# Row sums of the second norm one pair of weight pieces sooner, and two gate pieces loaded among the last projection's pieces

## The reference, cut to what matters

```
mod = silu(c) @ ada_w + ada_b                      # 6 x 1024: sh1, sc1, gt1, sh2, sc2, gt2
...
merged = gate_a * (o_a @ w_oa) + gate_b * (o_b @ w_ob)
x = x + gt1 * (merged @ w_out)
h = rms_norm(x, norm2_g) * (1 + sc2) + sh2
x = x + gt2 * hier_moe(h, router weights, w1, w3, w2)   # 32 experts, each token in 2 of them
out = rms_norm(x, final_norm_g)
```

## Time and profile before

| | |
|---|---|
| median of 3 runs | 700.7 us (698.7 to 700.85) |
| the profiled execution | 700.86 us, its span 699.0 us |
| granted TensorE clock, mean | 0.991 of 2.4 GHz |
| PE, PEld busy | 669.4 us (96%), 538.5 us (77%) |
| DVE, ACT, POOL busy | 420.1 us (60%), 264.8 us (38%), 71.4 us (10%) |
| HBM read | 195.35 MB |

### The profile page before, as it was taken

How to read it: one execution, slowest core, us unless ns; L and a number is a source line. 1 busy time by engine, 2 the same in 40 slices (tenths; PEclk the granted TensorE clock), 3 DMA queues, 4 the chain that set the end, 5 groups by cost and what they waited for, 6 DMA issues and landing times.

```text
span 699.0 us, 12784 instructions
## 1 busy us (share of the span) xinstructions
PE 669.4 (96%) x5402; PEld 538.5 (77%) x5402; DVE 420.1 (60%) x710; ACT 264.8 (38%) x373; POOL 71.4 (10%) x70
## 2 busy tenths in 40 slices
PE   8999999999999999999998999899999999999893
PEld 8999999998777777999988997675666666665441
DVE  4656788987866789977786678644333122221226
ACT  3346545557763624335552332312131121221003
POOL 0001000000003614300000000001112111111111
PEclk9999999999999999999999999999999999999998
DMA  8987764455343443346639976999999999999992
GB/s 363 423 353 243 298 248 175 130 177 191 121 157 130 161 142 121 122 140 253 241 108 397 410 280 249 423 421 418 419 397 418 421 421 421 419 418 418 420 355 95
DMA packets 31195, 201.23 MB, mean 288 GB/s; under 512 B 5047, under 2 KB 5431, under 8 KB 7970
## 3 DMA queue, kind: packets, MB, share of 16 engines
q1 hardware_dynamic: 27378, 193.27, 70.7%
q0 software_dynamic: 3760, 7.14, 2.8%
HBM read 195.35 MB, written 10.75 MB: 295 GB/s over the span
## 4 chain that ended last, share of the span: by engine, by line
PE 77%; DVE 9%; DMA 6%; ACT 3%; issue 2%; SPq 2%; DVEq 0%; POOL 0%; ACTq 0%; POOLq 0%
PE ps L1571 75%; DMA ring<-in_expert_pieces 4%; DVE ring_rounded L934 2%; DMA ring<-in_pieces 2%; ACT ring_rounded L644 2%; SPq L461 1%; PE ps L1988 1%; PE ps L1692 1%; DVE r_ct L1209 1%; DVE r_v L1209 1%; DVE r_xs_rounded L1239 1%; ACT sq L760 1%; DVE g_sb L1142 0%; DVE r_kq L1173 0%; DVE newton L920 0%
## 5 line engine op out<-in xcount | busy, mean ns | idle before, releaser
L934 DVE TENSOR_TENSOR ring_rounded<-ring,ring_rounded 128x2048 fp32r<-128x2048 f32 x60 | 136.8, 2291 | 38.8 <-ACT ring_rounded L644 38.5
L1571 PE MATMUL ps<-hT_rounded,ring_rounded 128*128 128x256 f32 x832 | 150.1, 286 | 1.1 <-ACT hT_rounded L658 1.1
L1571 PEld LDWEIGHTS ps<-hT_rounded,ring_rounded 128*128 128x128 f32 x832 | 129.2, 193 | 5.1 <-issue 3.9
L644 ACT CAST ring_rounded<-ring 128x2048 fp32r<-128x2048 f32 x60 | 114.1, 1906 | 34.4 <-PE ps L1571 18.8
L1571 PE MATMUL ps<-ring_rounded,hT_rounded 128*128 128x512 f32 x352 | 109.7, 393 | 0.9 <-DVE ring_rounded L934 0.9
L1571 PE MATMUL ps<-x_sb_rounded,ring_rounded 128*128 128x256 f32 x416 | 109.8, 284 | 0.0
L1571 PEld LDWEIGHTS ps<-x_sb_rounded,ring_rounded 128*128 128x128 f32 x416 | 77.3, 193 | 0.9 <-issue 0.2
L1571 PEld LDWEIGHTS ps<-ring_rounded,hT_rounded 128*128 128x128 f32 x352 | 64.3, 188 | 14.8 <-issue 1.4
L858 ACT ACTIVATE sq<-ps 128x128 f32<-128x128 f32 x32 | 8.9, 277 | 142.6 <-PE ps L1571 142.6
L1454 DVE TENSOR_TENSOR r_st<-ps,r_kq 128x512 f32<-128x512 f32 x32 | 22.1, 692 | 65.0 <-PE ps L1571 65.0
L603 POOL DMA_INDIRECT y_rows<-r_st,r_btm x29 | 28.5, 984 | 311.4 <-DVE r_st L1454 298.6
(11 more groups left out here) (336 smaller groups left out, 1002.9 us busy)
## 6 DMA issues: line engine op xcount, KB each, us to landing
ring<-in_pieces SPq DMA_DIRECT2D x66, 1024.0 KB, 5.0
ring<-in_expert_pieces SPq DMA_DIRECT2D x48, 1024.0 KB, 17.5
r_z<-in_expert_pieces SPq DMA_DIRECT2D x12, 1024.0 KB, 13.3
r_xs<-in_expert_pieces SPq DMA_DIRECT2D x12, 1024.0 KB, 12.5
r_v<-in_pieces SPq DMA_DIRECT2D x6, 1024.0 KB, 7.2
r_ct<-in_pieces SPq DMA_DIRECT2D x6, 1024.0 KB, 5.6
g_sb<-in_expert_pieces SPq DMA_DIRECT2D x6, 1024.0 KB, 17.2
r_st<-in_expert_pieces SPq DMA_DIRECT2D x6, 1024.0 KB, 17.9
```

The source lines that it names most:

```text
L644: nc.scalar.copy(high_of(p_), slot_of(p_)).then_inc(hi_ok, 1)
L934: nc.vector.tensor_tensor(low_of(p_), slot_of(p_), high_of(p_).bitcast(F32), ALU.subtract).then_inc(lo_ok, 1)
L1571: return nc.tensor.matmul(o, l, r, start=start, stop=stop)
```

## The change

Two things. DVE sums row pair 9 after the drain of `ob (1,0)` instead of `ob (1,1)`, and SP loads it accordingly when `ob (0,1)` has been read instead of `ob (1,0)`. And SP issues the first two gate pieces ahead of the load that waits for piece (1,0,1) of `ob`, which is that of `out` piece (1,0), instead of behind expert pieces 4 and 5.

```
-ROWS_AT = {("oa", 1, 1): 7, ("ob", 0, 1): 8, ("ob", 1, 1): 9}
+ROWS_AT = {("oa", 1, 1): 7, ("ob", 0, 1): 8, ("ob", 1, 0): 9}
...
-                if n >= LOADS and PIECES[n - LOADS] in (("ob", 0, 0, 1), ("ob", 1, 0, 1)):
+                if n >= LOADS and PIECES[n - LOADS] in (("ob", 0, 0, 1), ("ob", 0, 1, 1)):
                     piece_used(sp, PIECES[n - LOADS])
-                    load_rows(8 + PIECES[n - LOADS][1])
+                    load_rows(8 + PIECES[n - LOADS][2])
+                if n >= LOADS and PIECES[n - LOADS] == ("ob", 1, 0, 1):
+                    sp.wait_ge(start_row_read, 4 + len(ROW_PIECES))
+                    for p_q in GATE_ROWS[:2]:
+                        sp.dma_start(slot_of(p_q), piece_src(p_q)).then_inc(s_gate, 16)
                 load_piece(n, p_)
...
             load_moe(4)
             load_moe(5)
-            sp.wait_ge(start_row_read, 4 + len(ROW_PIECES))
-            for p_ in GATE_ROWS[:2]:
-                sp.dma_start(slot_of(p_), piece_src(p_)).then_inc(s_gate, 16)
             for p_ in GATE_ROWS[2:]:
                 load_piece(PIECE_AT[p_], p_)
...
                         if (name, i, h) in ROWS_AT:
-                            if (name, i) == ("ob", 1):
-                                before((("out", 0), 0))
+                            if name == "oa":
+                                split_to(SPLIT_AT["ob", 0, 0, 1] + 1)
                             rows_out(ROWS_AT[name, i, h])
```

## The result

Twelve runs of each kernel, in turn on one chip: 699.42 us before (698.32 to 702.1), 701.81 us after (700.46 to 703.78). The ratio is 1.0035, 95% interval 1.0022 to 1.0047: slower by 2.4 us (1.5 to 3.3). The forecast was no difference that can be measured, 700.5 us; 701.81 lies in its range, but the likeliest case was wrong. Two figures ahead of the result mislead a little: the median of three shown for before, 700.7, was 1.3 us above the one of twelve, and the profiled execution of before, 700.86 us, was 1.4 us above it. It lost TensorE's clock once more than that of after, from 60 to 68 us (granted 0.67 and 0.90 in two windows of 4 us, where after has 1.00). So after's profiled execution is 2.2 us ahead at 384 us (TensorE resumes at 383.55, in before at 385.72), and both spans are 699.0 us: the 2.2 us ahead are gone at the end.

What follows compares the result with a forecast made beforehand. The expert-weight stream was taken to set the end. TensorE 2.6 us late against 2.9 in hand gave -0.3 us on the profiled 700.86, and with the median 0.16 below the profiled time, 700.5; 8-in-10 range 697.6 to 703.4.

Steps and rivals of the forecast that it cites:

- 5.53 us at the router weights: DVE, before scaling the router weights: predicted to stand 5.0 us until their load lands at 429.8.
- 3.58 us at O3: TensorE, last projection's third piece: predicted to idle 3.6 us until DVE has split it at 433.7.
- the clock's fall: TensorE's granted clock, predicted to fall after the 3.6 us idle in the last projection, costing about 1.4 us.
- the new DMA hole before piece 16: Expert stream at some 465 to 468 us: earlier loads mostly given back as a hole before piece 16.
- how late TensorE is: TensorE's entry to the experts: predicted 2.6 us late, 1.2 plus 1.4 for the clock.
- the start of O4's half: TensorE's work on the last projection's fourth piece: predicted to start at 440.0 instead of 438.87, 1.2 us late.
- the stream had only 2.9 us in hand: Expert stream at piece 16: 2.9 us of slack on TensorE, so 2.6 us lateness gives -0.3 us.
- TensorE, not the stream, sets the end: Rival on the program's end: TensorE's 2.6 us lateness counts in full, 703.3 us; chance 0.05.
- not a step later: Rival: router weights land a burst step later, at 433.2, 3.4 us later; 703.8 to 705.1 us; chance 0.14.
- DVE did wait for them: Rival: router weights come early or don't hold the third piece's split; stream gains 3.8 us, 696.9; chance 0.12.
- the clock did fall: Rival: TensorE's clock stays up after its idle in the last projection; -1.7 us, 699.0; chance 0.21.
- its 3.4 us to spare: TensorE in the last experts: 3.4 us to spare against the stream, predicted to hold its 2.6 us lateness.

Runs made afterwards that it cites:

- 40 extra: The kernel before with 40 extra fp32 128x128 matmuls at TensorE's entry to the experts (8.95 us delay); measured +9.9 us (+8.2 to +11.7).
- 20 extra: The kernel before with 20 extra fp32 128x128 matmuls at TensorE's entry to the experts (4.5 us delay); measured +4.4 us (+2.9 to +5.9).
- gates behind, split first (6): Changed kernel, gate pieces issued behind the router weights and DVE splitting the last projection's third piece before scaling the router weights; 697.64 us, ratio 0.9973.
- gates behind (6): Changed kernel with the two gate pieces issued behind the router weights, ahead of expert pieces 4 and 5; 698.65 us, ratio 0.9959.
- rows only (3): The change's first half alone: pair 9 loaded and summed sooner, gate pieces back in their old place; 697.91 us, ratio 0.9972 to the kernel before.
- router weights first (1): Changed kernel with SP issuing the router weights ahead of the two gate pieces; 698.82 us, ratio 0.9982 to the kernel before.
- both cures (7): Changed kernel with router weights issued ahead of the gate pieces and the last projection's third piece split before the router scaling; 699.91 us, ratio 0.9998.
- split first (2): Changed kernel with DVE splitting the last projection's third piece ahead of the router weights' scaling; 699.75 us, ratio 0.9997 to the kernel before.
- 8 extra: The kernel before with 8 extra fp32 128x128 matmuls at TensorE's entry to the experts (1.8 us delay); measured +0.4 us (-0.8 to +1.7).
- 14 extra: The kernel before with 14 extra fp32 128x128 matmuls at TensorE's entry to the experts (3.1 us delay); measured +3.0 us (+1.7 to +4.3).
- wait filled (4): Changed kernel with 18 extra small matmuls on TensorE ahead of its wait for the last projection's third piece; 701.76 us, ratio 1.0022 to the kernel before.

## Why the prediction was wrong

**What held.** Pair 9's sums, the gate pieces' release and the waits came within a few tenths of a us, once the head start of 2.2 us is taken off: 5.53 us at the router weights (5.0 forecast), 3.58 us at O3 (3.6), the clock's fall, the new DMA hole before piece 16, the missing wait at the transposes. By the Trainium skill (TensorE: Matmul & The Clock Gate, "What's actually happening") the clock might have been spared; this trace has it fall.

**A small miss: how late TensorE is.** I had 2.6 us. The forecast's own numbers give 1.1 for the start of O4's half, not 1.2, and 1.5 for the fall of the clock, not 1.4; its sum, 700.86 - 0.3 - 0.16, is 700.4, not 700.5. The fifth piece of the long burst comes 1.3 us late by the rows, not 1.0. None of this changes the case. From the resumption at 385.72 to the first matmul of the selection (457.76) the kernel before takes 72.04 us, the changed one 458.71 - 383.55 = 75.16: 3.1 us. Half a us too little. The runs with 8 and 40 extra matmuls, the same code up to there, take 72.0 and 72.1 us without the extra work; those with 14 and 20 take 74.7, because the clock was lower on the way. So the 3.1 us hold for executions that keep the clock alike.

**The step that failed: "the stream had only 2.9 us in hand".** I read this off one piece, number 16, the first that needs a slot from TensorE (issued 464.51, landed 7.8 later instead of 4.9), and let the whole lateness be swallowed by it. That was the wrong reading: what the stream has in hand against a ring of slots is not what the first turn shows; it is the least over all turns. SP's queue shows TensorE's pace in handing out slots. First, in before, the rows with piece 16 and with pieces 32 and 33 (the second of an x2 row starts 0.33 before the row's end):

```profile
464.51 2.06 SPq L461 DMA_DIRECT2D r_z<-in_expert_pieces  x2
...
503.32 6.66 SPq L461 DMA_DIRECT2D r_z<-in_expert_pieces  x2
```

and in after the row with pieces 32 and 33, 0.96 us later, as TensorE's start is:

```profile
504.28 6.66 SPq L461 DMA_DIRECT2D r_z<-in_expert_pieces  x2
```

Piece 33 goes out at 509.65 before. From 464.51 that is 17 pieces in 45.1 us, 2.65 us each; a turn of a later expert takes 6.7 us for three, 2.23 each. What makes the first ones longer I did not take apart. The stream needs 2.5 each. So the 2.9 us shrink by 17 x 0.15 = 2.6, to an estimated 0.3 at piece 33. Its landing gives 1.2: 6.1 us after the issue, over the 4.9 of a piece alone. The trace with 40 extra matmuls gives a third value: there piece 33 went out 7.64 us later than before (517.29) and landed 5.5 us after that, 7.0 later than before, which makes 0.6. No single trace settles the size. With 8, 14 and 20 extra matmuls the piece landed 6.2, 6.1 and 6.0 us after its issue, in the changed kernel 6.9, so in these almost nothing was made up. The traces say that little of the 2.9 us was left; how little, the timed runs say: 0.1 to 0.8 us. The DMA issues of piece 33, in before:

```profile
r_z<-in_expert_pieces SPq DMA_DIRECT2D x1, 1024.0 KB, 6.1
```

and with 40 extra matmuls:

```profile
r_z<-in_expert_pieces SPq DMA_DIRECT2D x1, 1024.0 KB, 5.5
```

From piece 33 on the stream sets the pace and cannot make up a lost us: in the kernel before the DMA engines have a share of 1.01 or 1.02 in each of five windows of 24 to 30 us from 516 to 660 us, for instance

```profile
540.00:570.00 30.00, 30.00 (x251) 18.87 (x249) 6.44 (x20) 6.43 (x15) 3.92 (x4) 1.00 1.02 420
```

With 0.1 to 0.8 in hand the sum becomes 3.1 less that, +2.3 to +3.0 us; measured +2.4 (1.5 to 3.3). That the middle value of 0.6 gives +2.5 is closer than the readings allow, and partly luck.

The thirteen profiled executions show the same tie. For each: the first matmul of the selection, the issue of piece 33, the end of the span, all in us:

| kernel | selection | piece 33 | span | span less selection |
|---|---|---|---|---|
| gates behind, split first (6) | 454.13 | 506.04 | 695.2 | 241.1 |
| gates behind (6) | 455.82 | 507.73 | 697.1 | 241.3 |
| rows only (3) | 456.01 | 507.90 | 696.7 | 240.7 |
| router weights first (1) | 456.40 | 508.31 | 697.4 | 241.0 |
| both cures (7) | 457.02 | 508.93 | 697.8 | 240.8 |
| split first (2) | 457.33 | 509.23 | 698.7 | 241.4 |
| before | 457.76 | 509.65 | 699.0 | 241.2 |
| 8 extra | 458.05 | 509.93 | 698.6 | 240.5 |
| after | 458.71 | 510.61 | 699.0 | 240.3 |
| 14 extra | 462.01 | 513.89 | 702.5 | 240.5 |
| wait filled (4) | 463.17 | 515.08 | 704.9 | 241.7 |
| 20 extra | 463.31 | 515.19 | 705.0 | 241.7 |
| 40 extra | 465.41 | 517.29 | 706.8 | 241.4 |

TensorE starts the selection over a range of 11.3 us, piece 33 follows after 51.9 in every one, and the span ends 240.3 to 241.7 us after the start. (The starts hold what happened upstream too, so they are not the delays of the table above: before lost 2.2 us at 60 to 68 us, and the run with 20 lost some to a fall of the clock at 436 to 444 us.) Over this range, whatever hastens or delays TensorE's start at the experts moves the end by about as much. Differences under some 1.5 us can't be read from single executions: after starts the selection 0.95 us later than before, and both spans are 699.0.

**The rivals.** "TensorE, not the stream, sets the end", given 0.05 and priced at +2.6, had the size right and the place wrong: the chain still ends in an expert piece issued at 634.52 and 27.7 us under way. My argument against it, that the chain ends in the stream, says who is waited for last. It does not say who sets when the stream may start, and a stream that starts late ends late. TensorE still has its 3.4 us to spare at the end, in the turns of the last experts; it is the hand-over at the start of the stream that has almost none. The other rivals did not come: the router weights landed as forecast and not a step later, DVE did wait for them, and the clock did fall.

**A chance not seen.** The half of the change that moves pair 9 brings 2.0 us by itself (experiment 3). I had the parts of this (the 2.39 us wait that goes, O3's split no longer behind the sums), but never summed the two halves apart, and so did not see that one gained and the other lost.

**What stays open.** What a fall of the clock costs was not isolated by experiment 4, though traces of the same code give it for one stretch (below). The size of what the stream has in hand is known only as 0.1 to 0.8 us. Which of the three versions of experiments 3 and 6 is best was not settled either.

## What to carry to other kernels

Where a stream fills a ring of slots that an engine empties, what it has in hand is the least over all turns: compare the engine's pace per slot with the stream's, and follow it to the turn where the queue is shortest, not only the first. A change that reorders loads is best summed half by half, and a small late load (here 162 KB) is to be placed by who stands behind its waiter, not by its size. The chain's last link names the last to be waited for; to find what a delay costs, delay that engine alone and look.

## What the hardware showed beside

- The same wait does not always cost the clock. TensorE's wait of 2.39 us up to 438.46 left it at 1.00 in the kernel before; in the run with 20 extra matmuls, whose code is the same up to there, the wait is 2.39 again and the clock falls:

```profile
436.00:440.00 4.00, 1.98 (x7) 1.79 (x8) 2.12 (x4) 1.76 (x4) 0.00 (x0) 0.73 1.02 430
440.00:444.00 4.00, 4.00 (x16) 3.20 (x16) 0.92 (x2) 0.00 (x0) 0.00 (x0) 0.84 1.01 426
```

The Trainium skill (TensorE: Matmul & The Clock Gate, "What's actually happening") says that the beat on which the clock is judged is not tied to the kernel. This pair agrees with that and does not prove it.

- The same pair prices such a fall. From the transposes behind the wait to the next ones TensorE has the same work; it takes 446.14 - 438.46 = 7.68 us in before and 447.21 - 438.02 = 9.19 us with 20 extra matmuls, so the fall cost 1.5 us. The next transposes, first in before, then both in the run with 20:

```profile
446.14 1.07 PE L1692 MATMUL ps<-par,x_sb 128*128 128x128 f32 x8
...
438.02 1.11 PE L1692 MATMUL ps<-par,x_sb 128*128 128x128 f32 x4 [2.39 <-DVE x_sb L1287]
447.21 1.07 PE L1692 MATMUL ps<-par,x_sb 128*128 128x128 f32 x8
```

- The clock also fell with almost no wait recorded before. With the gate pieces behind the router weights, TensorE idled 0.54 us at 443.8, and then:

```profile
444.00:448.00 4.00, 4.00 (x24) 2.51 (x26) 3.37 (x19) 0.26 (x1) 0.00 (x0) 0.80 1.01 416
448.00:452.00 4.00, 4.00 (x16) 1.21 (x14) 3.27 (x14) 2.19 (x2) 0.00 (x0) 0.77 1.00 418
```

Such falls come and go between executions of much the same code. With the split first as well, TensorE idled 0.55 us at 443.83 before the same 16 matmuls of the router, and the clock stayed at 1.00. The next group of six matmuls started 7.67 us after them there, and 9.37 us after them in the run shown: this fall cost 1.7 us. Runs of one kernel differ by some us, and lower clocks go with longer times: over the 35 runs of before that were timed with experiments 1 to 4 and the 29 timed with the runs of 8 and 14, time and mean granted clock are correlated by -0.72 and -0.80, with 0.4 to 0.5 us for each 0.001 of the clock.
